# Copying the value pages to a DRAM scratch beside the input projection, and finer alternation in the attention stage

## The reference, cut to what matters

```python
past_s = tuple(jnp.take(cache_nsa_kv[l, :, :, c], page_table, axis=0)...)   # k_cmp, v_cmp, k_sel, v_sel
...
s = einsum('bqkgd,bkqmd->bkgqm', q, k_sel[selected]) * ATT_SCALE + bias
p = masked_softmax(s, mask)
o = einsum('bkgqm,bkqmd->bqkgd', p, v_sel[selected])
```

## Time and profile before

| | |
|---|---|
| median of 3 runs | 3050.29 us (3049.18 to 3064.09) |
| the profiled execution | 3046.35 us, its span 3044.6 us |
| PE busy | 2620.6 us, 86% of the span |
| granted clock of TensorE, mean | 0.891 |
| projection, both layers (from the span's start) | 53 to 226.6, 1553 to 1727.3 us |
| attention, both layers | 530.5 to 753.5, 2025 to 2244.5 us |

### The profile page before, as it was taken

The page is one execution under the profiler, slowest core; times in us unless marked ns, Lnnn a source line. Parts: engine busy times, 40 slices in busy tenths (PEclk is TensorE's granted clock), DMA queues, the critical chain, the costliest instruction groups (busy, mean ns, idle before and its releaser), DMA issues. The chain is left out here.

```text
span 3044.6 us, 44769 instructions
## 1 busy us (share of the span) xinstructions
PE 2620.6 (86%) x17428; PEld 2139.6 (70%) x17428; DVE 872.8 (29%) x1901; ACT 565.9 (19%) x1180; POOL 238.2 (8%) x328
## 2 busy tenths in 40 slices
PE   6996999645698999999969879977458989999997
PEld 4875887533585888888758668855347758888885
DVE  2732333612544210000118223344134332000002
ACT  0013322411420210000110223323032103000002
POOL 0500000000030100000006000000002101000000
PEclk8997999767695999999979989988677669999998
DMA  6205774152001134023042267742400020341220
GB/s 195 74 28 158 222 225 149 59 142 74 2 22 45 46 100 136 28 61 78 1 137 70 49 204 224 219 126 67 129 25 1 21 91 29 108 127 28 56 56 30
DMA packets 343603, 277.01 MB, mean 91 GB/s; under 512 B 61473, under 2 KB 339106, under 8 KB 343002
## 3 DMA queue, kind: packets, MB, share of 16 engines
q1 hardware_dynamic: 307624, 249.51, 27.8%
q10 hardware_dynamic: 35762, 24.57, 2.7%
HBM read 264.16 MB, written 18.17 MB: 93 GB/s over the span
## 5 line engine op out<-in xcount | busy, mean ns | idle before, releaser
L2250 PE MATMUL psum<-xT,up_ring 128*128 128x272 f32 x2048 | 470.3, 392 | 0.0
L2250 PEld LDWEIGHTS psum<-xT,up_ring 128*128 128x128 f32 x2048 | 389.1, 190 | 80.3
L2269 PE MATMUL psum<-ff,HT 128*128 128x272 f32 x1536 | 353.6, 392 | 0.0
L2269 PEld LDWEIGHTS psum<-ff,HT 128*128 128x128 f32 x1536 | 291.8, 190 | 60.2
L368 PE MATMUL psum<-xT,w_ring 128*128 128x272 f32 x1408 | 329.0, 397 | 5.5 <-PEq L162 4.0
L368 PEld LDWEIGHTS psum<-xT,w_ring 128*128 128x128 f32 x1408 | 270.8, 193 | 63.6 <-issue 4.7
L979 PE MATMUL psum<-cst,cache 128*128 128x128 f32 x1600 | 208.1, 285 | 17.7 <-DMA cache<-in_cache_nsa_kv 11.5
L979 PEld LDWEIGHTS psum<-cst,cache 128*128 128x128 f32 x1600 | 178.2, 145 | 40.5 <-DMA cache<-in_cache_nsa_kv 12.6
L2113 DVE SCALAR_TENSOR_TENSOR xT<-xT,psum 128x544 f32<-128x544 f32 (+1 forms) x42 | 24.2, 585 | 528.8 <-PE psum L2269 441.6
L1009 PEld LDWEIGHTS psum<-chunks,W 64*128 64x128 f32 x2304 | 132.1, 189 | 16.9 <-ACT st_sel L1089 11.7
L1009 PE MATMUL psum<-chunks,W 64*128 64x128 f32 (+1 forms) x2304 | 138.7, 276 | 0.0
(11 more groups left out here) (428 smaller groups left out, 3096.5 us busy)
## 6 DMA issues: line engine op xcount, KB each, us to landing
cache<-in_cache_nsa_kv SPq DMA_DIRECT2D x512, 192.0 KB, 2.8
up_ring<-in_w_up SPq DMA_DIRECT2D x32, 1024.0 KB, 5.3
HT<-in_w_down SPq DMA_DIRECT2D x12, 2048.0 KB, 9.0
w_ring<-in_w_in SPq DMA_DIRECT2D x20, 1024.0 KB, 4.8
W<-in_cache_nsa_kv SPq DMA_DIRECT2D x160, 64.0 KB, 1.9
p_sel<-in_cache_nsa_kv SPq DMA_DIRECT2D x160, 64.0 KB, 1.9
HT<-in_w_out SPq DMA_DIRECT2D x8, 1024.0 KB, 6.0
yT<-in_w_down SPq DMA_DIRECT2D x4, 2048.0 KB, 11.0
```

The source lines that it names most:

```text
L2250: last = pe.matmul(psum[:, 2 * (t % 4) + h, 0:HALF], up_ring[:, g % 3, k, (t % 2) * P:(t % 2) * P + P], xT[:, k, half_of(h)], start=(k == ...
L2269: last = pe.matmul(psum[:, 2 * (t % 4) + h, 0:HALF], down[t % 3][:, k, :], f[:, k, half_of(h)], start=(k == 0), stop=(k == FT - 1))
```

## The change

The stage `proj` gets a new job for SP. Behind the weight load of each of the groups 2 to 9, SP issues the copies of 32 value pages (one sequence) from the cache to a scratch in DRAM, `v_dram`, in which the 16 pages of a half lie side by side in each of 128 rows. At the stage's end SP waits for all 256 of them. In the attention stage SP loads a half with one DMA of 1 MB, and ACT fetches nothing. A step "t" is now one half (16 steps in place of 8), and the order alternates steps and units until the units are out: halves 0 to 11 stand beside rounds, and halves 12 to 15 behind the last of them. Nothing is changed in what is computed.

```diff
+def value_pages(S, l, sp, first, n, sem):
+    io, half = S.io, NPG // 2
+    for f in range(first, first + n, 8):
+        for j, page in enumerate(page_numbers(S, mybir.EngineType.SP, f // NPG, f % NPG, 8)):
+            src = layer(io.cache_nsa_kv, l)[ds(page, 1)].rearrange("a t c k d -> (a t) (c k d)")
+            at = f % NPG + j
+            sp.dma_start(io.v_dram[f // NPG, at // half, :, at % half, :], src[:, 3 * P:4 * P]).then_inc(sem, 16)
...
                 load(sp, g, g % slots, loaded[g % slots])
+                if "sync" in more:
+                    more["sync"](sp, s, g)
+            if "sync_end" in more:
+                more["sync_end"](sp, s)
...
+    def sync(sp, s, g):
+        if 2 <= g < 10:
+            value_pages(S, l, sp, (g - 2) * NPG, NPG, s.values)
+
+    def sync_end(sp, s):
+        sp.wait_ge(s.values, 16 * NB * NPG)
...
-        if k < n_top - 4:
+        if k + 4 < n_chain + n_values:
             order += ["t"]
...
-    n_top = 9 + NG + NB + 1
-    order = attention_order(n_top, N + 4, NB)
-    by_sp = 10
+    order = attention_order(9 + NG, N + 3, 2 * NB)
...
-                fetch(sp, mybir.EngineType.SP, hh, 0, by_sp, pages[hh % 4])
+                sp.dma_start(vsel[hh % 4][:, :, :], io.v_dram[b, hh % 2]).then_inc(pages[hh % 4], 16)
...
                     for h in range(2):
                         hh = 2 * b + h
-                        pe.wait_ge(pages[hh % 4], 16 * by_sp * (hh // 4 + 1))
-                        pe.wait_ge(more[hh % 4], 16 * (half - by_sp) * (hh // 4 + 1))
+                        pe.wait_ge(pages[hh % 4], 16 * (hh // 4 + 1))
                         for t in range(half):
...
                         last.then_inc(s.part, 1)
-                    yield
+                        yield
...
             def sample():
-                fetch_rest(0)
-                fetch_rest(1)
                 yield
...
-                    if p == NG - 1:
-                        act.wait_ge(s.pt_turned, NG)
-                        fetch_rest(2)
-                        fetch_rest(3)
                     yield
-                for b in range(NB):
-                    if 2 * b + 4 < 2 * NB:
-                        act.wait_ge(s.part, 2 * b + 1)
-                        fetch_rest(2 * b + 4)
-                        act.wait_ge(s.part, 2 * b + 2)
-                        fetch_rest(2 * b + 5)
-                    if b % 2 == 0:
-                        act.wait_ge(s.part, 2 * b + 2)
+                for hh in range(2 * NB):
+                    if hh % 4 == 1:
+                        act.wait_ge(s.part, hh + 1)
...
+    args["v_dram"] = nc.dram_tensor("v_dram", (NB, 2, P, NPG // 2, P), F32, kind="Internal").ap()
```

More of the change, by code:

```diff
@@ L537, in gpsimd @@
         keep_tails(S, pool, s)
-    more = {"vector": vector, "gpsimd": gpsimd, T_GLU + 1: sigmoid}
+    def sync(sp, s, g):
[3 more added lines that the diff above has]
+        sp.wait_ge(s.values, 16 * NB * NPG)
+    more = {"vector": vector, "gpsimd": gpsimd, T_GLU + 1: sigmoid, "sync": sync, "sync_end": sync_end}
     for j in range(6):
@@ L550, in project_in @@
           lhsT, N_IN, evac_act, evac_dve, beside=keep_window, ready=1, on_dve=on_dve, more=more,
-          more_names=("sigmoid", "placed", "taps", "moved", "packed", "psteps", "pooled", "g_taps", "g_conv", "g_kept", "g_swish"))
+          more_names=("values", "sigmoid", "placed", "taps", "moved", "packed", "psteps", "pooled", "g_taps", "g_conv", "g_kept", "g_swish"))
 def page_numbers(S, engine, b, first, n):
@@ L1163, in in_turn, with attention_order @@
             pass
-def attention_order(n_top, n_units, n_values):
+def attention_order(n_chain, n_units, n_values):
     order = ["t"] * 4
@@ L1216, in attention @@
              "s_turned", "placed", "window", "strip",
-             "pages0", "pages1", "pages2", "pages3", "more0", "more1", "more2", "more3",
+             "pages0", "pages1", "pages2", "pages3",
              "scored", "biased", "cstep", "c_maxed", "c_exped", "coef", "normed", "turned", "pt_copied", "pv", "o_act", "o_dve")
     with stage(nc, "att", *names) as (block, s):
-        pages, more = (s.pages0, s.pages1, s.pages2, s.pages3), (s.more0, s.more1, s.more2, s.more3)
+        pages = (s.pages0, s.pages1, s.pages2, s.pages3)
         def width(n):
@@ L1228, in blocks @@
             return 1 if br == 0 else i + 1
[L1230 to L1234, removed]
         @block.sync
@@ L1378, in _ @@
         def _(act):
-            def fetch_rest(hh):
-                fetch(act, mybir.EngineType.Activation, hh, by_sp, half - by_sp, more[hh % 4])
             def copy_vc(i):
@@ L1414, in sample @@
                         act.copy(dst, psum[:, p % 3, :].rearrange("p (t n) -> p t n", n=P)).then_inc(s.pt_act, 1)
-                    if p == NG - 1:
-                        act.wait_ge(s.pt_turned, NG)
-                        fetch_rest(2)
-                        fetch_rest(3)
                     yield
-                for b in range(NB):
-                    if 2 * b + 4 < 2 * NB:
-                        act.wait_ge(s.part, 2 * b + 1)
-                        fetch_rest(2 * b + 4)
-                        act.wait_ge(s.part, 2 * b + 2)
-                        fetch_rest(2 * b + 5)
-                    if b % 2 == 0:
-                        act.wait_ge(s.part, 2 * b + 2)
+                for hh in range(2 * NB):
+                    if hh % 4 == 1:
+                        act.wait_ge(s.part, hh + 1)
                         act.wait_ge(s.vc, 4)
-                        act.copy(o_s[:, b, :], psum[:, b % 3, 0:P]).then_inc(s.s_act, 1)
+                        act.copy(o_s[:, hh // 2, :], psum[:, hh // 2 % 3, 0:P]).then_inc(s.s_act, 1)
                     yield
@@ L1526, in sample @@
                     yield
[L1527 to L1530, removed]
+                for hh in range(2 * NB):
+                    if hh % 4 == 3:
+                        dve.wait_ge(s.part, hh + 1)
+                        dve.tensor_copy(o_s[:, hh // 2, :], psum[:, hh // 2 % 3, 0:P]).then_inc(s.s_dve, 1)
                     yield
```

## The result

The changed kernel takes 3070.93 us in the median of 18 runs, the kernel before 3055.53 us in 18 (the three runs shown before are among them). The ratio is 1.0046, 95% interval [1.0033, 1.006]: about 14 us slower (the two medians are 15.4 apart), where 2972 us was forecast. The profiled executions are 3075.03 us with a span of 3073.3, against 3046.35 and 3044.6.

A forecast was written before the change was run, and what follows sets the result against it. TensorE work was taken to bound the projection, SP's page issue the end of attention. From 3046.35 us, 150 off for attention and 72 added for projection gave 2968, with 4 for the median 2972; range 2930 to 3050, 8 in 10.

The forecast's parts named there:

- What bounds the stage: End of attention: PE waits 63.9 us for value pages because SP's issuing is long; a half at most every 8.3 us.
- The attention stage, 75 us a layer: Gain forecast for attention: 66.5 us at its end plus 8.9 at its start, 150 us in all.
- The last part, from half 10 to the barrier: End of attention: 20 us for the last round and halves 11 to 15, 5 us for fold, last copies and barrier.
- The window load's wait: Attention: sequence b's window load waits for the first half of sequence b - 1, with half 2b queued behind it.
- so I take 0.333: Projection: issuing a page copy from DRAM to DRAM costs 0.333 us, as into SBUF; 0.527 kept for the range.
- The prediction's own sign of being wrong: Projection: a page step of 0.8 us or more on SP, where 0.65 us was forecast.
- The start of the stage, 5 us of hold-up: Projection: pages behind the first two weight loads wait for room while ACT's copies fill the DMA engines; 5 us, between 0 and 14.
- The other projection terms: Projection's end: group 10's weights land 4.8 us after issue, two tiles 14.7, last tile 7.5, 2.5 for a PE that stood still.
- B: Rival, projection: DRAM-to-DRAM issue costs ACT's 0.527 us, total 3071; gain used up at 0.485; chance 0.15.
- C: Rival, attention: rounds take 7.4 us as engines' turns come late and the clock stays low, total 3014; chance 0.12.
- E: Rival, projection: DMA engines take longer than SP's issue, 0.75 us a page, 51 us more, total 3023; chance 0.06.
- D: Rival, projection: copies' issues fit between the weight loads and PE waits for nothing, total 2900; chance 0.05.

The follow-up runs named there:

- Experiment 8: Experiment 1's kernel with one page-table read for all pages of a half on each queue, in place of one for two pages: 2992.45 us, ratio 0.9804.
- Experiment 1: The kernel before with only the change's order (steps of half a sequence), pages still fetched one by one by SP and ACT: 3029.32 us, ratio 0.9922.
- experiment 5: The changed kernel with the old order, a value step being a whole sequence again, copies and 1 MB loads kept: 3083.27 us, ratio 1.0115.
- Experiment 3: The changed kernel with the copies in two hops, each page loaded into SBUF and eight stored to the scratch with one DMA: 3040.03 us, ratio 0.9949.
- Experiment 6: The changed kernel with ACT's eight window copies issued late in the projection, one behind each tile from 12 on: 3060.8 us, ratio 1.0032.
- experiment 7: The changed kernel with projection weight loads on ACT and the copies shared, 168 on SP and 88 on ACT: 2876.92 us, ratio 0.9432.
- experiment 4: The changed kernel with the projection's weight loads issued by ACT and the 256 copies alone on SP: 2995.79 us, ratio 0.981.

## Why the prediction was wrong

- **What bounds the stage**: right. The pace of the value steps was the issue of pages. Experiment 8 shortens the issue alone, and the stage follows. Experiment 1 leaves the issue, and the stage stays.
- **The attention stage, 75 us a layer**: it gave 87.6 and 83.8. The start gained 9.0 us as worked out: PE's first held-up step comes 5.6 us into the stage, against 14.6. From there to half 0 another 4.6 us went (58.6 against 63.2), for which the sum had nothing; no run takes that stretch apart. The rounds took 4.5 us, not 5.3, and the clock is part of the difference: 0.96 in 702 to 745 us, where the value steps stand, against 0.66 before. Idle PE had cost twice, in waits and in clock. The last part, from half 10 to the barrier, took 25.6 us, with 25 predicted: the last halves began 7.0 and 9.6, then 5.9 and 8.4 us after the release of their buffers, where 6 and 9 had been put down, twice. The window load's wait behaved as described, and experiment 5 shows what it costs once nothing stands between the sequences.
- **The step that failed is "so I take 0.333".** The price of a copy's issue was 0.493 us. The nearest row by kind of transfer (ACT's 0.527, DRAM to DRAM) was set aside for the nearest by shape (128 rows, 0.333), and here the kind was the better guide. 0.16 x 512 = 82 us of the miss come from it. A weight load's step is 27.1 us where 21.3 were worked out: 5.1 are this price, the other 0.7 are smaller extras, such as the weight load's own instruction (0.44 us in place of 0.37). Experiment 3 shows the price by itself. The prediction's own sign of being wrong, a page step of 0.8 us or more, is what the timeline shows (0.80).
- **The start of the stage, 5 us of hold-up**: 13 us (39.45 against 26.36). The range 0 to 14 had it near its end; the middle was no estimate. That is 16 us more for two layers. Together, a layer: 41 us from the price, 8 from the hold-up, 6 from the extras. The projection costs 92 us where 36 were forecast. Experiment 6 shows that the term isn't removed by moving its cause.
- **The other projection terms** held. Group 10's weights landed 5.7 us after issue (4.8), the first group after a wait ran 16.4 us (14.7 + 2.5), the last tile 7.5.
- **The rivals.** B, the dearer issue, is what happened, with a price of 0.493 in place of 0.527; its turning point of 0.485 was just passed. It had a chance of 0.15, and the range was drawn to leave its full size out. That its total of 3071 us is the measured one is luck: the price was lower than B's, the hold-up and the extras (27 us for two layers) were in no rival, and the attention stage gave 21 us more. C (rounds of 7.4 us) and E (engines slower than the issue, at 0.75 us a page) are refuted: the rounds took 4.5 us, and in experiment 7 the engines moved 256 pages in 172 us, 0.67 us a page, beside the weights. D asked for PE to wait for nothing. In the changed kernel it waits 9 to 15 us a group. **The sentence of the Trainium skill** (DMA: Bandwidth & Descriptors, "Issuing engines are not separate DMA queues"), that sequencer time is usually small relative to the DMA, does not hold here: in the changed kernel SP issued without a pause while the DMA engines were busy 0.40 of the time, and sharing the issue between two queues, experiment 7, took some 94 us a layer out of the projection with the same bytes moved.

## What to carry to other kernels

Count small DMAs by their issue on the queue, address work and table reads included, and ask what else is issued behind them on it: 256 copies, beside which the DMA engines were busy 0.40 of the time, delayed the last weight load by 115 us (174.5 to 289.3). Look for a row that is alike in source and target as well as in shape before you take the price of an instruction from it. Neither alone gives it: in the kernel before, loads into SBUF of other shapes took from 0.37 (weights, L429) to 0.60 us and more (L795). Where two rows differ by 0.2 us and the count is 512, the choice is the forecast. Work moved to another stage must fit into the time that the issuing queue has free there: SP's queue was nearly empty for 174 us of projection, but 256 copies of 0.80 us and more need some 205. With ACT's 6 us a tile beside it they fit.

## What the runs showed that was not expected

- A DMA instruction for 128 rows of 512 bytes takes SP 0.333 us from DRAM into SBUF and 0.493 from DRAM into DRAM, in the median of 512 each; the store of 8 pages out of SBUF 0.42.
- A queue seems to fill. With two 1 MB weight loads ahead and ACT's copies on the engines, the first page's instruction stood 11.95 us (changed kernel) and 11.82 us (experiment 3). With ACT's copies moved (experiment 6) the first copy stood 1.3 us. With the weight loads on ACT's queue no copy stood so long: the longest stood 5.1 us (experiment 4) and 5.3 us (experiment 7), and it came some 10 us after the first copy. That a queue has room for so many pieces and no more is inferred from these times.
- The last part of the delta rule takes 14.7 or 22 us by the granted clock (1.00 or 0.57), with the same instructions, in one execution or another; the kernel before shows both in one. What decides it stays open. It is up to 15 us of 3050 from run to run, as much as the effect of this change.
